# Modulation chunks 3 and 4 on TensorE in column groups, and the attention's values products in two parts

## What is computed

```python
def modulation(cond, w_mod, b_mod):
    m = jax.nn.silu(cond) @ w_mod + b_mod
    return jnp.split(m[:, None, :], N_MOD, axis=-1)

def trunk_layer(x, cond, ctx_k, ctx_v, p):
    sh1, sc1, gt1, sh2, sc2, gt2 = modulation(cond, p['w_mod'], p['b_mod'])
    h = rms_norm(x, p['norm1_g']) * (1.0 + sc1) + sh1
    q, k, v, u = mixer_projections(h, p['w_in'], p['q_norm_g'], p['k_norm_g'])
...
    pooled = pool_mixer(u, p['w_pool'], p['pool_scale'])
    mix = jnp.concatenate([attn, pooled.astype(attn.dtype)], axis=-1) @ p['w_out']
    x = x + gt1 * mix
    h2 = rms_norm(x, p['norm2_g']) * (1.0 + sc2) + sh2
    x = x + gt2 * conv_ffn(h2, p['w_up'], p['conv_w'], p['conv_b'], p['w_down'])
    return x, new_k, new_v
```

## Time and profile before

| | us |
|---|---|
| median of 3 runs | 1502.22 |
| lowest and highest | 1500.97, 1504.16 |
| profiled execution | 1499.22 |
| its span, first to last instruction | 1497.4 |
| outside the span | 1.8 |

### The profile page before, as it was taken

How to read it: one execution, slowest core, us unless ns; L and a number is a source line. 1 busy time by engine, 2 the same in 40 slices (tenths; PEclk the granted TensorE clock), 3 DMA queues, 4 the chain that set the end, 5 groups by cost and what they waited for, 6 DMA issues and landing times.

```text
span 1497.4 us, 25179 instructions
## 1 busy us (share of the span) xinstructions
PE 1427.3 (95%) x10013; PEld 1382.7 (92%) x10013; DVE 942.9 (63%) x1410; ACT 517.0 (35%) x742; POOL 398.1 (27%) x259
## 2 busy tenths in 40 slices
PE   7987889999999999999999979999999999999996
PEld 4987679999999999999999967999999999999996
DVE  3997995799784658794854778339944323444323
ACT  3335672343222123323132567324322212332321
POOL 0274001124441014343214500122433101323320
PEclk9999899999999999999999989999999999999998
DMA  9541112425434424344512200132422321222321
GB/s 337 181 129 31 57 58 74 153 79 160 126 116 141 152 89 149 114 126 125 157 54 71 75 1 1 34 108 73 132 78 79 94 67 58 83 70 71 97 59 70
DMA packets 191870, 147.05 MB, mean 98 GB/s; under 512 B 4384, under 2 KB 179112, under 8 KB 190760
## 3 DMA queue, kind: packets, MB, share of 16 engines
q1 hardware_dynamic: 190592, 145.32, 31.5%
q10 hardware_dynamic: 1192, 0.52, 0.1%
HBM read 142.94 MB, written 2.88 MB: 97 GB/s over the span
## 4 chain that ended last, share of the span: by engine, by line
PE 82%; DVE 9%; issue 3%; ACT 2%; POOL 1%; DMA 1%; SPq 0%; DVEq 0%; ACTq 0%; POOLq 0%
PE pair L1169 69%; PE pair L1186 4%; DVE mod_acc L845 3%; PE pair L1451 2%; PE pair L1429 2%; PE pair L1416 2%; DVE small L1054 1%; PE pair L1256 1%; DVE w_lo L822 1%; POOL tree L486 1%; PE pair L1287 1%; DMA xin<-in_x_sample_dram 1%; ACT tree L732 1%; PE pair L1239 0%; DVE conv L1113 0%
## 5 line engine op out<-in xcount | busy, mean ns | idle before, releaser
L1169 PE MATMUL pair<-in_hi,w_hi 128*128 128x320 f32 x1792 | 411.6, 311 | 10.0 <-DVE w_lo L822 10.0
L1169 PE MATMUL pair<-in_hi,w_lo 128*128 128x320 f32 x1792 | 409.1, 310 | 0.0
L1169 PE MATMUL pair<-in_lo,w_hi 128*128 128x320 f32 x1792 | 409.0, 310 | 0.0
L1169 PEld LDWEIGHTS pair<-in_hi,w_hi 128*128 128x128 f32 x1792 | 299.9, 188 | 11.9 <-issue 8.8
L1169 PEld LDWEIGHTS pair<-in_lo,w_hi 128*128 128x128 f32 x1792 | 300.3, 188 | 0.0
L1169 PEld LDWEIGHTS pair<-in_hi,w_lo 128*128 128x128 f32 x1792 | 300.1, 188 | 0.0
L1113 DVE SCALAR_TENSOR_TENSOR conv<-pair,vec,conv 128x127 f32<-128x127 f32 x352 | 168.7, 541 | 200.4 <-ACT conv L760 200.3
L517 POOL TENSOR_TENSOR silu_a<-silu_a,conv 128x640 f32<-128x640 f32 x44 | 110.8, 2519 | 561.2 <-DVE conv L1113 561.2
L822 DVE TENSOR_TENSOR w_lo<-w_raw,w_hi 128x1024 fp32r<-128x1024 f32 (+1 forms) x152 | 203.4, 1339 | 41.7 <-ACT w_hi L538 41.5
L538 ACT ACTIVATE w_hi<-w_raw 128x1024 fp32r<-128x1024 f32 (+1 forms) x88 | 103.2, 1173 | 353.8 <-PE pair L1169 323.7
L845 DVE SCALAR_TENSOR_TENSOR mod_acc<-mod_raw,cond,mod_acc 128x1024 f32<-128x1024 f32 x140 | 221.6, 1624 | 0.0
(11 more groups left out here) (164 smaller groups left out, 1547.7 us busy)
## 6 DMA issues: line engine op xcount, KB each, us to landing
w_raw<-in_w_up_dram SPq DMA_DIRECT2D x88, 512.0 KB, 3.9
mod_raw<-in_w_mod_dram SPq DMA_DIRECT2D x80, 512.0 KB, 3.9
w_raw<-in_w_down_dram SPq DMA_DIRECT2D x32, 704.0 KB, 4.6
w_raw<-in_w_in_dram SPq DMA_DIRECT2D x20, 512.0 KB, 4.0
w_first<-in_w_mod_dram SPq DMA_DIRECT2D x8, 1024.0 KB, 14.6
w_raw<-in_w_out_dram SPq DMA_DIRECT2D x16, 512.0 KB, 4.2
out_dram<-yout SPq DMA_DIRECT2D x5, 512.0 KB, 3.9
xin<-in_x_sample_dram SPq DMA_DIRECT2D x4, 512.0 KB, 6.6
```

What stands on the lines that cost most here:

```text
L1169: ins = pe.matmul(dst[:, a:a + HALF_T], w[:, s, k, :], rhs[:, kk, a:a + HALF_T], start=first and r == 0, stop=last and r == 2)
```

## The change

Chunks 2 and 3 are made by TensorE in the way of chunks 0 and 1. A new function `mod_second` does the product of a row block of both chunks. The eight products stand in the input projection of layer 0: k = 0 after the pair of tiles, k = 1 after the third tile, k = 2 to 5 after tiles 3 to 6 and k = 6 and 7 after tile 7. The sums gather in the second bank of `pair3`, so the statistics of the keys move from `lin[3]` to `lin[2]`. The row blocks, 1 MB each, are loaded into the places of `mod_raw` and `mod_acc` in turn, and `cond_cols` moves to `ssum`. VectorE's units of chunks 2 and 3 are gone, with their partial sums and reductions. Independently of this, `weigh_pair` gets a second argument: the products of key tiles 0 to 2 of a pair run at even i, those of tiles 3 and 4 at the following odd i, in both layers.

```diff
+            def load_second(k):
+                if k == 0:
+                    sp.wait_ge(s_xsq, NT)
+                elif k == 1:
+                    sp.wait_ge(s_ft, 1)
+                else:
+                    sp.wait_ge(s_second, k - 1)
+                sp.dma_start(second_place[k % 2], w_mod[0, k * P:(k + 1) * P, 2 * D:4 * D]).then_inc(s_sld[k % 2], 16)
...
-                    for k in units_at.get(n, ()):
-                        load_mod(2, k, k % 2)
...
+                    if L == 0 and 1 <= n < NK - 1:
+                        load_second(n + 1)
...
+                    if L == 0 and n == NK:
+                        act_e.wait_ge(s_second, NK)
+                        act_e.activation(second_rows, pair[3][:, 512:1024], ACT.Copy).then_inc(s_srow, 1)
...
-                units_at = {0: (0, 1), 1: (2, 3), 2: (4,), 3: (5,), 4: (6,), 5: (7,)} if L == 0 else {}
...
-                    for k in units_at.get(n, ()):
-                        mod_unit(2, k, k % 2)
-                    if L == 0 and n == 5:
-                        mod_part_sums(2)
+                    if L == 0 and n == N_IN - 1:
+                        mod_finish(2)
+                        mod_finish(3)
...
-                    if L == 0 and i % 2 == 0 and 4 <= i < 4 + 4 * NK:
-                        k = i // 4 - 1
-                        mod_unit(3, k, k % 2, (i % 4 // 2,))
-                    if L == 0 and i == 4 + 4 * NK:
-                        mod_part_sums(3)
...
-                    if L == 0 and m == 1:
-                        mod_finish(3)
...
+            def mod_second(k):
+                pe.wait_ge(s_sld[k % 2], 16 * (k // 2 + 1))
+                for j in range(4):
+                    ins = pe.matmul(pair[3][j * QUAD:(j + 1) * QUAD, 512:1024], cond_cols[:, k, :],
+                                    second_place[k % 2][:, j * 512:(j + 1) * 512], start=k == 0, stop=k == NK - 1)
+                ins.then_inc(s_second, 1)
...
+                    if L == 0 and n < NK:
+                        mod_second(n - 1)
+                        if n == NK - 1:
+                            mod_second(n)
+                    if L == 0 and n == NK:
+                        pe.wait_ge(s_srow, 1)
+                        for t in range(4):
+                            ins = pe.transpose(pair[3][:, 512 + t * P:512 + (t + 1) * P], second_rows[:, t * P:(t + 1) * P], ident)
+                        ins.then_inc(s_st, 1)
...
-                    for kt in range(nkt):
+                    for kt in range(min(nkt, 3)) if part == 0 else range(3, nkt):
...
-                for i in range(NU + 3):
-                    if i >= 4 and i % 2 == 0:
-                        weigh_pair(i - 4)
+                for i in range(NU + 4):
+                    if i >= 4:
+                        weigh_pair(i - 4 - i % 2, i % 2)
```

58 lines of the change are left out of this document (30 added, 28 removed).

## The result

| | before | after |
|---|---|---|
| median, us | 1503.19 (4 runs, 1500.97 to 1505.29) | 1484.18 (4 runs, 1483.23 to 1485.4) |
| profiled execution, us | 1499.22 | 1485.40 |
| its span, us | 1497.4 | 1483.6 |
| mean granted clock | 0.983 | 0.987 |

The ratio is 0.9874, with an interval of 0.9859 to 0.9889: the change takes 19.0 us off, between 16.7 and 21.2. The prediction of 1486 us, in a range of 1480 to 1495, held. Two numbers in the table don't agree, though: the medians differ by 19.0 us, the two profiled executions by 13.8 us. The forecast had added up -15.7 us. So the size of each term has to be looked at, and the part of the time that no term names.

What follows compares the result with a forecast made beforehand. TensorE, busy for 95% of the span, was taken as the bound. The terms -11.4 - 0.7 + 2.2 - 5.8 = -15.7 us, set against the 1502.2 us median, gave 1486 us, in a range of 1480 to 1495 us.

Steps and rivals of the forecast that it cites:

- projection of layer 0: Layer 0's input projection: 86.84 + 9.2 + 0.5 + 0.4 + 1.0 = 97.9 us against 95.72 us, so +2.2 us.
- attention of layer 0, VectorE's work gone: Layer 0's attention loses 16 accumulations and a partial sum on VectorE and falls to layer 1's time, -11.4 us.
- attention of layer 0, split: Layer 0's attention: values products in two parts cover TensorE's wait for ScalarE's copy, -2.9 us.
- output projection of layer 0, without its norm: Layer 0's output projection: without chunk 3's small sums ahead of chunk 4's units, a 1.21 us TensorE wait shrinks, -0.7 us.
- attention of layer 1, split: Layer 1's attention: the same split of the values products, 2.5 us in 13 pairs plus 0.4 us at the end, -2.9 us.
- The stalls of the projection: Layer 0's input projection: TensorE's waits for `w_lo` (6.8 us) and the slow clock behind (2.1 us) go; rival they stay, 0.04.
- The products: Layer 0's input projection: eight column-group products between tiles, seven places at 1.18 us and one at 0.99 us, 9.2 us.
- the last load: Layer 0's input projection: the k = 7 load of 1 MB lands slightly late, 1.0 us lost, bounds 0 and 8 us.
- groups that run one after another: Rival, layer 0's input projection: column groups between full-width tiles don't run together, +30 us, 1517 us; chance 0.01.
- a clock that falls with each product: Rival, layer 0's input projection: column groups bring TensorE to 1.2 GHz, tiles behind take 14.1 us, +49 us, 1536 us; chance 0.02.
- the split wins the whole wait: Rival, both attentions: the whole 0.53 us wait per pair is won, 8.9 us more, 1478 us; chance 0.04.
- a split without gain: Rival, both attentions: ScalarE's or VectorE's chain is the pair's next limit, 4.2 us stay, 1492 us; chance 0.13.

Runs made afterwards that it cites:

- products alone: The changed kernel with the values products of a pair in one piece again, leaving only the products in column groups: 1488.91 us, ratio 0.9908.
- The short products: The changed kernel with the products of row blocks 1 to 7 over 32 of 512 columns a group: 1482.62 us in one run.

## Why the prediction held, point by point

| term | forecast, us | measured in the stages, us |
|---|---|---|
| projection of layer 0 | +2.2 | +0.7 |
| attention of layer 0, VectorE's work gone | -11.4 | -11.8 (products alone) |
| attention of layer 0, split | -2.9 | -2.3 (the rest of -14.1) |
| output projection of layer 0, without its norm | -0.7 | -0.2 |
| attention of layer 1, split | -2.9 | -2.5 |
| sum (of unrounded times) | -15.7 | -16.0 |
| three norms, in the profiles | 0 | +1.2 |
| everything else, in the profiles | 0 | +1.0 |

The sum came out 0.3 us from its forecast because errors cancel: the projection cost 1.5 us less than forecast, while the split and the output projection gave 1.5 us less and VectorE's freed work 0.4 us more. No single term is off by more than 1.5 us, but the closeness of the sum is in part luck.

**The stalls of the projection.** The waits for `w_lo` are gone. This is all that TensorE's matmuls waited for between 41 and 138 us, to be set beside the earlier trace rows:

```profile
PE pair L1418 <- DVE in_lo L1021: 1.1, 2, 0.9
PE pair L1192 <- ACT in_hi L637: 0.5, 1, 0.5
```

That the accumulations made the waits is shown by the run that shortened only them.

**The products.** The chain of that projection, two places, the last load, and the transposes and small adds:

```profile
55.96 0.99 PE pair L1300 x8
56.95 7.23 PE pair L1192 x48
64.18 1.00 PE pair L1300 x8
65.18 7.23 PE pair L1175 x48
...
102.54 6.48 DMA mod_acc<-in_w_mod_dram
...
109.07 1.06 PE pair L1300 x8
...
118.38 0.49 PE pair L1393 x4
...
133.20 0.39 DVE mod L887 x4
```

Product and tile together take 8.23 us against 7.05 us of a tile alone: 1.18 us, as worked out from the fillers in the earlier trace rows. The transposes (0.49 us) and the adds (0.39 us, on the chain) are as forecast. The rival of groups that run one after another (30 us) and that of a clock that falls with each product (49 us) are refuted by these rows; the granted clock of the stretch is 0.99.

**A mis-sized term: the last load.** Forecast: data there 12.1 us after tile 6, TensorE asks after 11.1 us, 1.0 us lost. Tile 6 ends at 98.2 us. The load is issued at 102.54 us, 4.3 us later (4.4 forecast), and the product starts at 109.07 us, 10.9 us later (11.1 forecast). Those two were right. The landing took 6.48 us, where 5.8 + 1.9 = 7.7 us had been estimated for 1 MB with the 512 KB ahead of it. So the data were there after 10.8 us and not after 12.1 us, just as the product ahead of it ended (109.02 us), and nothing that can be seen was lost. The slope of the earlier trace rows was fair for the 1 MB: the last five of these loads, each issued behind a weight tile of 512 KB, landed after 6.1 to 6.5 us, against 5.8 us. The 1.9 us for the weight tile ahead were too much on top of it. Only two transfers were under way, not three. The stage as a whole moved 172 GB/s, more than the 136 GB/s that the prediction had estimated. The short products show how little slack there is. Layer 1's own projection, the base of the sum, is 0.3 us shorter in this trace (86.52 us), which is most of the rest of the difference: 86.5 + 9.2 + 0.5 + 0.4 = 96.6 us, measured 96.4 us, just under the 97 to 98 us that the prediction had named as its sign.

**The attention of layer 0.** Taking layer 1 as a measurement of layer 0 without VectorE's extra work was right to 0.4 us. The prediction spoke of 16 accumulations and a partial sum in one breath. The runs show that the one instruction weighs nearly as much as all the others (4.9 us, with the accumulations already shortened).

**The split.** A pair after the change, weight loads as in the earlier trace rows:

```profile
895.43 0.20 PEld L1476 LDWEIGHTS pair<-prob_t,past 128*64 128x64 f32 x4 [0.17 <-issue]
896.24 0.19 PEld L1440 LDWEIGHTS pair<-k_hi,q_st 128*128 128x128 f32 x1 [0.17 <-issue]
897.57 0.42 PEld L1476 LDWEIGHTS pair<-prob_t,val 128*64 128x64 f32 x8 [0.17 <-issue]
898.16 0.19 PEld L1440 LDWEIGHTS pair<-k_hi,q_st 128*128 128x128 f32 x1 [0.17 <-issue]
899.49 0.20 PEld L1476 LDWEIGHTS pair<-tree,past 128*64 128x64 f32 x4 [0.17 <-issue]
```

From 895.43 to 899.49 us is 4.06 us; it was 4.20 us, and 4.01 us was forecast. The 0.53 us wait is gone and two switches of 0.17 us have come, so 0.14 us a pair are won where 0.19 us were expected. The fair comparison for layer 1 is the kernel with the products alone, since both kernels take 14.31 us there from the first scores to the first values product, where the kernel before takes 13.42 us. Against it the attention is 2.87 us shorter, the 2.9 us that were forecast, but made up otherwise: nine steady pairs give 1.3 us, the four pairs ahead of the short block and that block 1.0 us, and the end 0.6 us. Forecast were 13 x 0.19 = 2.5 us and 0.4 us. The rule of the Trainium skill, TensorEngine Tiling (Array Packing), section Key Properties, that a change of the tiling mode drains TensorE, agrees with these rows: four switches of 0.17 us a pair where there were two. The rival that the split wins the whole wait fell by that.

The last pair waits 0.20 us for its copy, where it was 0.79 us:

```profile
929.58 0.44 PE L1476 MATMUL pair<-tree,past 128*64 128x128 f32 x4 [0.20 <-ACT tree L747]
```

VectorE and ScalarE, the next that could bind, still wait in each pair. Where it was once a pair, 0.93 and 1.01 us, it is now twice: 0.46 and 0.24 us for VectorE, 0.35 and 0.57 us for ScalarE. The longer of VectorE's and the shorter of ScalarE's:

```profile
901.19 0.82 DVE L1067 TENSOR_REDUCE small<-pair 128x1 f32<-128x640 f32 x1 [0.46 <-PE pair L1440]
899.60 0.70 ACT L747 ACTIVATE prob_t<-pair 128x640 f32<-128x640 f32 x1 [0.35 <-PE pair L1453]
```

So TensorE is the bound, and the rival of a split without gain is refuted. In sum 0.70 and 0.92 us of room are left in a pair.

**The output projection of layer 0.** Here the mechanism was wrong. The wait of 1.21 us is still there after the change:

```profile
271.00 0.53 PE L1175 MATMUL pair<-in_hi,w_hi 128*128 128x320 f32 x2 [1.25 <-DVE w_lo L837]
```

The 0.71 us of chunk 3's sums stood at the start of chunk 4's units (249.41 us in the earlier trace rows), and taking them out didn't reach the wait, which comes 34 us later. What is gained is 0.2 us: without its norm the stage takes 58.24 or 58.25 us in the six kernels with chunk 3 on VectorE and 58.07 to 58.09 us in the seven others. TensorE's folding of chunk 3's sums is gone from it, two instructions behind which the next matmuls started 0.43 us after the last in place of 0.29 us.

**What the sum did not name.** The norms and the start, with 2.1 us against the change in the profiled pair, and some 3 us for it in the medians (19.0 against 16.0 us). The prediction set the profiled execution (3.0 us under the median) beside the medians as if the distance were the same for both kernels. After the change the profiled execution is 1.2 us above its median. So the measured 1484.2 us lie 2 us under the forecast 1486 us not by the terms, which sum to within 0.3 us, but by what they leave out.

## What to carry over

Where two layers run the same code and only one carries extra work on a helper engine, their difference is a price list for that work, waits and clock included, and no model is needed. Weigh a helper's instruction by where it stands and how long it is in one piece, not by its share of the sum: 2.3 us in front of a unit's maximum cost 4.9 us, the same 2.3 us in front of a tile's low part left 0.3 us of wait. And before a profile's difference is read as a change's worth, sum what the change doesn't touch, and cut stages so fine that nothing untouched lies within them: here a norm at another clock made -1.4 us out of a term of -0.2 us.

## What I had not expected of the hardware

- The granted clock falls to its lower level (1.2 GHz) in the norms with no longer idle stretch ahead than 0.86 us, and once with none of over 0.2 us (0.74 over 13 us, TensorE busy for 12.91 us, with ten matmuls of one column and short fillers). The same code runs at 1.00 in other executions. A norm takes 7.3, 8.5 to 8.8 or 10.06 us, so this costs up to 2.8 us a norm.
- Fillers in a waiting stretch at the start of layer 0's attention moved the fall of the clock to the next stretch instead of preventing it (0.76 and 1.00 became 0.92 and 0.77).
- A product in four column groups between full-width tiles still costs 0.39 us when its columns are cut from 512 to 32: 0.20 us of the eight matmuls and 0.19 us in the tile behind.
- A load of 1 MB issued right behind one of 512 KB landed after 6.1 to 6.5 us (five loads of the kernel after), 8.8 and 10.9 us with four and more others issued beside it; in the full queue at the start it took 14.6 us.
